# Spreading reciprocal roots by transposes, and storing eight table rows 128 times instead of computing them 128 times

## What is computed

```
def rmsnorm(a, g):
    af = a.astype(jnp.float32)
    af = af * lax.rsqrt(jnp.mean(af * af, axis=-1, keepdims=True) + EPS)
    return (af * g.astype(jnp.float32)).astype(a.dtype)
...
        _, idx = lax.top_k(score, topk)
...
        bias = rel_bias[t5_bucket(idx - qpos[None, :, None])]
        logits = logits + jnp.transpose(bias, (0, 3, 1, 2)).astype(jnp.float32)
```

## Time and profile before

| | |
|---|---|
| median of 3 runs | 2641.26 us (2639.55 to 2644.37) |
| span of the profiled execution, first to last instruction | 2643.9 us, 2.6 us above the median and within the runs shown |
| PE, DVE, POOL, ACT busy | 97%, 48%, 47%, 40% |
| mean granted TensorE clock | 0.992 of 2.4 GHz |
| DMA | 238.48 MB, 90 GB/s on average |

### The profile page before, as it was taken

How to read it: one execution, slowest core, us unless ns; L and a number is a source line. 1 busy time by engine, 2 the same in 40 slices (tenths; PEclk the granted TensorE clock), 3 DMA queues, 4 the chain that set the end, 5 groups by cost and what they waited for, 6 DMA issues and landing times.

```text
span 2643.9 us, 35252 instructions
## 1 busy us (share of the span) xinstructions
PE 2575.0 (97%) x12632; PEld 2144.7 (81%) x12632; DVE 1281.3 (48%) x2488; ACT 1046.5 (40%) x1957; POOL 1240.6 (47%) x865
## 2 busy tenths in 40 slices
PE   8999999999999999999998999889999999999999
PEld 7888887787888888887877777779878888888887
DVE  4115445277766663225356777667327333333222
ACT  5335553243333332214255666477334333332120
POOL 2132223455666665444524544264245666666441
PEclk9999999999999999999999999999999999999999
DMA  4233212312222235210312122221312222226311
GB/s 153 72 96 92 89 65 95 144 57 91 78 85 83 81 135 207 80 64 15 114 65 85 57 72 72 77 92 33 136 64 72 87 86 78 86 80 239 112 48 72
DMA packets 89262, 238.48 MB, mean 90 GB/s; under 512 B 10208, under 2 KB 22784, under 8 KB 88704
## 3 DMA queue, kind: packets, MB, share of 16 engines
q1 hardware_dynamic: 89088, 236.21, 25.6%
HBM read 180.60 MB, written 51.38 MB: 88 GB/s over the span
## 4 chain that ended last, share of the span: by engine, by line
PE 79%; DVE 5%; issue 2%; ACT 2%; DMA 1%; POOL 1%; SPq 0%; ACTq 0%; DVEq 0%; POOLq 0%
PE PS L936 9%; PE PS L934 9%; PE PS L935 9%; PE PS L688 7%; PE PS L690 7%; PE PS L689 7%; PE PS L953 6%; PE PS L952 6%; PE PS L954 6%; PE PS L1209 2%; PE PS L816 2%; PE PS L1189 1%; PE PS L791 1%; PE PS L1174 1%; PE PS L1175 1%
## 5 line engine op out<-in xcount | busy, mean ns | idle before, releaser
L688 PE MATMUL PS<-Hh,Wl 128*128 128x512 f32 x1072 | 440.9, 411 | 13.8 <-DVE Hl L1322 9.0
L690 PE MATMUL PS<-Hh,Wh 128*128 128x512 f32 x1072 | 423.4, 395 | 0.0
L689 PE MATMUL PS<-Hl,Wh 128*128 128x512 f32 x1072 | 422.9, 394 | 0.0
L3039 POOL TENSOR_TENSOR Wl<-Wr,Wh 128x1024 fp32r<-128x1024 f32 (+1 forms) x83 | 188.4, 2271 | 382.2 <-ACT Wh L2201 382.2
L3140 POOL TENSOR_TENSOR RG<-RW,RG 128x512 fp32r<-128x512 f32 x176 | 244.9, 1395 | 142.4 <-ACT RG L2475 142.4
L1698 DVE TENSOR_TENSOR XA<-PS,XA 128x512 f32<-128x512 f32 x192 | 132.4, 691 | 330.0 <-PE PS L954 330.0
L952 PE MATMUL PS<-Hh,RG 128*128 128x512 f32 x704 | 274.1, 389 | 1.1 <-POOL Hl L3234 0.7
L954 PE MATMUL PS<-Hh,RG 128*128 128x512 f32 x704 | 273.9, 389 | 0.0
L953 PE MATMUL PS<-Hl,RG 128*128 128x512 f32 x704 | 273.9, 389 | 0.0
L688 PEld LDWEIGHTS PS<-Hh,Wl 128*128 128x128 f32 x1072 | 206.1, 192 | 57.5 <-POOL Wl L3039 10.2
L935 PE MATMUL PS<-Hl,RG 128*128 128x512 f32 x640 | 249.0, 389 | 0.0
(11 more groups left out here) (354 smaller groups left out, 5160.6 us busy)
## 6 DMA issues: line engine op xcount, KB each, us to landing
RW<-in_wg SPq DMA_DIRECT2D x44, 512.0 KB, 3.6
RW<-in_wu SPq DMA_DIRECT2D x44, 512.0 KB, 4.5
R<-in_wd SPq DMA_DIRECT2D x88, 256.0 KB, 2.9
hgscr<-GB SPq DMA_DIRECT2D x44, 512.0 KB, 2.6
G<-hgscr SPq DMA_DIRECT2D x40, 512.0 KB, 6.7
Wr<-in_wi SPq DMA_DIRECT2D x27, 512.0 KB, 3.3
Wr<-in_wo SPq DMA_DIRECT2D x16, 512.0 KB, 3.2
spill<-X SPq DMA_DIRECT2D x16, 512.0 KB, 2.6
```

The lines of the kernel that those rows point to most:

```text
L688: pe.matmul(ps(b), k.Wl[:, s, wc], xh[:, kx, sl], start=kk == 0, stop=False)
L689: pe.matmul(ps(b), k.Wh[:, s, wc], xl[:, kx, sl], start=False, stop=False)
L690: i = pe.matmul(ps(b), k.Wh[:, s, wc], xh[:, kx, sl], start=False, stop=kk == nk - 1)
L3039: pool.tensor_tensor(k.Wl[:, s, 0:w], k.Wr[:, s, 0:w], k.Wh[:, s, 0:w].bitcast(F32), ALU.subtract).then_inc(*up("w_lo", "w_lo", u))
```

## The change

`spread` no longer multiplies by the identity but transposes the broadcast column. The position table is one product of all eight columns, which leaves head h's row on partition h; ACT copies 8 x 384 values once, and the store reads each of the eight rows 128 times, so that HBM gets what it got before. The waits for the eighth row become waits for the one. All else keeps its place in memory and in the lists.

```diff
@@ memory
-    k.RR, at = put("RR", [128, 8, 384], home)
+    k.RR, _ = put("RR", [8, 384], home)
+    at = home + 12 * T
@@ tensor: spread
-            m = pe.matmul(ps(b, 512)[:, 128 * i:128 * i + 128], r.to_broadcast([128, 128]), ident, start=True, stop=True)
+            m = pe.transpose(ps(b, 512)[:, 128 * i:128 * i + 128], r.to_broadcast([128, 128]), ident)
@@ tensor: relative
-    def relative(h):
-
-        b = (2, 7)[h % 2]
-        take(b)
-        if h == 0:
-            pe.wait_ge(*at("d_rb_in"))
-        pe.matmul(ps(b, 384), k.rb[:, h:h + 1].to_broadcast([32, 128]), k.rb[:, 8:392], start=True,
-                  stop=True).then_inc(*up(("full", b), "rel", h))
+    def relative():
+
+        take(2)
+        pe.wait_ge(*at("d_rb_in"))
+        pe.matmul(k.PS[0:8, 1024:1408], k.rb[:, 0:8], k.rb[:, 8:392], start=True, stop=True).then_inc(*up(("full", 2), "rel"))
@@ tensor and scalar: index_scores
-                if n < 8:
-                    relative(n)
+                if n == 0:
+                    relative()
@@ scalar: relative
-    def relative(h):
-        b = (2, 7)[h % 2]
-        act.wait_ge(*at("rel", h))
-        act.activation(k.RR[:, h, :], ps(b, 384), ACT.Copy).then_inc(*up(("free", b), "rel_out", h))
+    def relative():
+        act.wait_ge(*at("rel"))
+        act.activation(k.RR[:, :], k.PS[0:8, 1024:1408], ACT.Copy).then_inc(*up(("free", 2), "rel_out"))
@@ scalar: topk
-        act.wait_ge(*at("rel_out", 7))
+        act.wait_ge(*at("rel_out"))
@@ sync
-    sp.wait_ge(*at("rel_out", 7))
-    sp.dma_start(d["rscr"], k.RR[:, :, :]).then_inc(*up("d_rb", "rel_stored"))
+    sp.wait_ge(*at("rel_out"))
+    rows = k.RR.rearrange("p (a n) -> p a n", a=1).to_broadcast([8, 128, 384])
+    sp.dma_start(d["rscr"].rearrange("p h n -> h p n"), rows).then_inc(*up("d_rb", "rel_stored"))
```

## The result

The changed kernel takes 2647.77 us as a median of 20 runs (2643.70 to 2653.84), the kernel before 2643.49 on the same chips (20 runs, 2638.22 to 2648.53). The ratio is 1.002, 95% interval 1.0013 to 1.0026: slower by 3.4 to 6.9 us. The forecast was 2639.2, 2 us faster; its range held the time, its sign is wrong. One execution of a later kernel took 3219 us at a mean granted clock of 0.75, and all ratios are of the others.

The account below looks back on a forecast made before the run. The prediction took TensorE (PE) to bound the kernel. Spreads -5.4, table -7.9, PE held by the store +9.2 and lower clock +2 sum to -2.1 us, from median 2641.3 to 2639.2; range 2628 (less 1) to 2650.

Parts of the forecast that it names:

- What bounds the kernel: Whole kernel: TensorE (PE) bounds it, busy 97% of the span and 79% of the chain that ended last.
- The store: Position table's store from 8 partitions: 29 us of data instead of 6.0 us, issued about 1382.6, completion seen near 1415.
- the held PE: At the key statistic: PE stands from 1405.8 to 1415 because ScalarE waits for the table's store, costing 9.2 us.
- two extrapolations: Table's store: one measured halving of partitions carried over four, giving 66 GB/s (24 us) or 44 GB/s (35 us).
- CS late, and no cost: Cosine table load behind the store: lands near 1417, first rotation ends at 1425; nothing added, 0 to 2 us in range.
- I add 2 us once (0 to 4): After PE's 9 us stop at the key statistic: a lowered PE clock costs 2 us, range 0 to 4.
- Rows 3: Profile windows around the position table: PE idle 3.6 and 3.2 us in 1420 to 1460, granted clock 0.91.
- I take all of it: All 12 spreads: 0.45 us saved at each counts fully, 5.4 us in total, bounds 3 to 6 us.
- The table's 7.9 us: Position table on PE: seven products fewer save 7.3 us, the wait before the second iw_turn 0.58 us; together 7.9.
- elsewhere a cut on PE can be taken at face value: Outside 1420 to 1460 us, an instruction removed from PE's stream saves its full spacing.
- The hidden store: Rival, chance 0.31: engines limit the table's store to 209 GB/s, it lands before 1405.8, 13.3 us stays: 2628.

Follow-up runs that it names:

- every fourth partition: Changed kernel with each bias column laid out four times, so the store reads partitions 0, 4, ... 28; ratio 0.9974 to the kernel before, 6.9 us faster.
- the one kernel with eight transposes: Kernel before with each spread made of eight transposes, the four issued twice, in place of the fp32 products; ratio 0.9998 to the kernel before.

## Why the forecast was wrong

Its sum was -5.4 - 7.9 + 9.2 + 2 = -2.1 us; it came out as about -1.8 - 6.3 + 8.5 + 2.5 to 6.2, which is +3 to +7, with +5 measured. The other way to add it up puts all of the clock in one term: the spreads' 5.4 less the 1.4 that waits take back, the table's 6.3, the wait's 8.5 and an estimated 7 for the clock give -4.0 - 6.3 + 8.5 + 7 = +5.

- **What bounds the kernel** was right: PE, and around the table a chain over ScalarE.
- **The store** was right in place and size, and in that few partitions are read slowly: 32.3 us from issue to release, where the forecast has 1382.6 to 1415, 32.4 us; the held PE 8.4 to 9.3 us against 9.2. Both ends came some 1.4 us later than forecast, by the wait at `rep_q` that it lacked, and cancel. It took the middle of two extrapolations (24 and 35 us), and that it hit is in part luck; every fourth partition shows that the number of partitions, by which it extrapolated, isn't the cause. The citation beside it, two ports for partitions 0 to 7, is what held.
- **CS late, and no cost** from it: right. GpSimd took it 13 us later than before and the second rotation still waited 5.3 us for `rr`.
- **The clock, "I add 2 us once (0 to 4)"** is the step that failed most. Rows 3 were for stops of 1.9 and 3.2 us. One of 8.4 us had 24 us at 1.2 GHz in it and behind it, and cost 6.2 us in that trace, 2.5 in the table alone. Over the executions the clock of the whole kernel is an estimated 7 us, of which 2.6 are there with the spreads alone.
- **The spreads, "I take all of it"** failed too: 0.45 us of spacing each is right, but n1's pair was hidden behind DVE's IQl and half of conv's behind DVE's Hl, 1.4 us together; and shorter work near a stop went with the lower clock in ffn and, in four of seven profiles, in n1. That the shorter work is its cause rests on the one kernel with eight transposes. 1.8 us kept against 5.4, below the lower bound of 3.
- **The table's 7.9 us** was 6.3: "elsewhere a cut on PE can be taken at face value" overlooked that PE would catch up with ScalarE at `rep_q`.
- Three terms erred to the same side, together by 6 to 9 us; the sign went with them. The hidden store as a rival was wrong for this change, and is what every fourth partition makes of it (203 GB/s, its 209). Whether the eight partitions or half of the DMA engines limit the store there is open: no run tells them apart.

## What to carry to other kernels

A row that is repeated by a DMA is read from SBUF once for each copy (a quarter of the copies less was 6 us less): put its sources on partitions that are spread out, or store it once and repeat it from HBM to HBM. Here a gain of 5 to 7 us took the place of a loss of 5. Price a stop of TensorE with the clock behind it, by rows of stops as long, and take a cut on the bounding engine at face value only up to the next wait on another engine.

## What was not expected

The issue of the CS load took SyncE 8.73 us (0.33 before) while the store held its queues, and 3.18 us with every fourth partition: a slow DMA can hold up the issuing engine as well. It cost nothing here: the next issue came at 1399.45, 6.0 us earlier than before, as PE was. And half of PE's work taken out of a spread went with a drop of the engine's clock in the norm around it: in ffn the trace of the spreads alone went from 0.8 us ahead of before to 0.3 us behind it within 4 us. Of these 1.1 us, 0.9 came back at 617 us, where PE before waits 1.0 us for DVE and this one 0.1.
